# A transformer layer on one core: the first block's heads turned by VectorE instead of TensorE, and three pieces of work near the start given other places

## The chip, the cores and the metric

One core of a Trainium2 chip runs the whole kernel in one launch. The metric is the time of one execution on the device in microseconds (us). The engines are named as the profile names them: PE is TensorE (PEld its weight loads), DVE is VectorE, ACT is ScalarE, POOL is GpSimd, and SP is the sync engine, which here does nothing but issue most of the DMA transfers.

## The reference: what is computed

One decoder layer over 256 tokens of width 2048, in float32. After an RMSNorm, one wide input projection gives the columns of two attention groups: eight heads of sparse attention (queries, and keys and values for a compressed, a selected and a windowed branch, with sigmoid gates per head and branch) and four heads of differential attention. The part that matters here is the start of the first group:

```python
k_cmp = compress_blocks(apply_rope(k_c.reshape(b, t_len, g, dh), cos, sin), cmp_pos, cmp_k_w1, cmp_k_w2)
v_cmp = compress_blocks(v_c.reshape(b, t_len, g, dh), cmp_pos, cmp_v_w1, cmp_v_w2)
...
blocks = jnp.transpose(blocks, (0, 1, 3, 2, 4)).reshape(b, n_cmp, g, CMP_BLOCK * dh)
return jax.nn.silu(blocks @ w1) @ w2
```

Both groups' outputs are multiplied by a SiLU branch, concatenated, sent through an output projection and added to the input, and a final RMSNorm follows.

## The kernel before, in words

**The work as a stream.** The projections are cut into column blocks of 512, and each block into four chunks: a chunk is four 128 x 512 tiles of weights (1 MB). The weights of the two compressions (`ck`, `cv`) are cut in chunks of the same size. The list `STREAM` (lines 54 to 62) is the order in which PE takes all chunks; it is written out by hand, and everything else is placed by numbers that name a chunk of this list. Its beginning before the change, with the chunk number c: c0 to c7 are the chunks of input blocks 0 (`kc`, `vc`: keys and values to be compressed) and 1 (`ks`, `kw`: the two other branches' keys) mixed; c8 and c9 the first two chunks of block 2 (`vs`, `vw`: their values); c10 to c13 the first four chunks of `ck`; c14 and c15 the other two of block 2; c16 and c17 block 3; c18 to c21 the rest of `ck`.

**A projection chunk.** For each tile of weights `w` the kernel makes a rounded high part `whi` (ACT, line 487) and the rest `wlo = w - whi` (DVE, line 786), and PE adds up three products, `whi*x_hi`, `wlo*x_hi` and `whi*x_lo` (lines 1191 to 1193; lines 1230 to 1237 in the first five chunks), for two tiles of 128 tokens: 24 matmuls of 512 columns a chunk. PE takes a chunk only when its high and its low part are there (lines 1173, 1174). ACT and DVE each run one loop over c: in turn c they split the chunk two places further on in the list of projection chunks, so in turn 7 the one for c9, and in turn 8 the next after that (c14 before the change). There are four raw buffers and three split buffers; SP reloads a raw buffer when both parts of the chunk that was in it are made (lines 382, 383), in the order of the list `LOADS`. A compression chunk isn't split: 16 matmuls of 512 columns with 32 columns of weights each (line 1250), 0.9 us in place of 5.4 us.

**All engines keep to the order of their own program.** What stands in an engine's turn c runs in that order, and a wait holds up everything behind it on that engine.

**Block 0.** In turn 6 ACT takes its values into `stage` (line 530), DVE scales the sine and cosine tables by the token norm (line 1032) and takes the keys with rotary embedding in two parts (lines 838 to 841), and POOL adds the two parts (line 437, one instruction for each tile of tokens). After chunk 7 PE transposes the eight 128 x 128 squares into the PSUM banks `S` (line 1269), ACT copies them out to `kvcT` in turn 8 (line 545), and DVE adds the position vector to form `kblkf` in turn 8 and `vblkf` in turn 13 (line 1054), with which PE begins `ck` and `cv`.

**Block 1** is a head block: DVE applies the rotary embedding when it is done (turn 7 and the start of turn 8), POOL adds, and DVE turns its heads in turns 9 and 10 into `kaT` with 16 stream transposes of 32 rows (line 850); these wait for the gate products, since `kaT` lies where `xTs` was. **Block 2** holds values: ACT takes the high part (line 539), DVE the low one (line 910), after c15.

**The gates.** DVE forms `gw` from the gate weights `gwf` in turn 7 (line 1061), PE multiplies after c9 (line 1276, 32 small matmuls), ACT copies the result out (line 706).

Of the kernel before, what the change touches and what calls it, by code (L numbers as in the profile page):

```python
# [24 lines left out]
P = 128  # L25
D_MODEL, SEQ, HEAD = 2048, 256, 128
TT = SEQ // P
KT = D_MODEL // P
# [14 lines left out]
for _n, _w in (("qa", 1024), ("kc", 256), ("vc", 256), ("ks", 256), ("vs", 256), ("kw", 256), ("vw", 256),  # L43
# [3 lines left out]
N_GATE = 24  # L47
BLOCKS = [("kc", "vc"), ("ks", "kw"), ("vs", "vw"), ("qa", 0), ("qa", 1), ("qb", 0), ("kb", 0), ("qb", 1),
          ("kb", 1), ("vb", 0), ("vb", 1), ("za", 0), ("za", 1), ("zb", 0), ("zb", 1)]
# [6 lines left out]
STREAM = [("in", b, j) for b, j in ((0, 0), (1, 0), (0, 1), (1, 1), (0, 2), (0, 3), (1, 2), (1, 3))] + _in[8:9]  # L56
for _i in range(0, 16, 4):

    STREAM += _in[9 + max(_i - 3, 0):10 + _i] + _cmp[_i:_i + 4]
STREAM += _in[22:24]  # L60
# [9 lines left out]

ROPE = [0, 1, 3, 4, 5, 6, 7, 8]
HEADS_AT = {b: {0: 7}.get(b, LAST["in", b] + 2) for b in ROPE}
Z = [11, 12, 13, 14]
# [3 lines left out]
SQ = 32  # L77
GATE_AT, GATE_TURN = 9, 17
CMP_SCORES_AT, CMP_PROBS_AT = 39, 45
# [43 lines left out]
def program(nc, stream, w_gate, head, x, norm_w, cmp_pos, ck_w2, cv_w2, lam, subln_w, final_w, consts, out):  # L123
# [3 lines left out]
    with ExitStack() as ctx:  # L127
# [134 lines left out]
        rope_ready = sem("rope_ready")  # L262
        kvc_turned, kvc_taken = sem("kvc_turned"), sem("kvc_taken")
        heads_turned, z_turned = sem("heads_turned"), sem("z_turned")
# [23 lines left out]
        READERS = {b: "v" for b in range(N_IN + N_OUT)}  # L288
        READERS.update({0: "vs", 2: "sv", 9: "sv", 10: "sv", 11: "s", 12: "s", 13: "s", 14: "s"})

# [4 lines left out]
        def values(b, t):  # L295

            at = slice(0, NB) if b == 2 else slice((b - 9) * NB, (b - 8) * NB)
            return [m[:, t, at] for m in ((va, va_lo) if b == 2 else (vb, vb_lo))]

# [177 lines left out]
        def _(act):  # L477
# [55 lines left out]
            def take_v(b, t):  # L533

                a = use_done(b, t)
                if b == 9:
                    act.wait_ge(scores_done, TT * N_A)
                dst = values(b, t)[0]
                act.activation(dst, a[:, :], ACT.Copy, scale=rstd[:, t:t + 1]).then_inc(acc_read["s"], 1)

            def take_kvc():

                for t in range(TT):
                    act.wait_ge(kvc_turned, t + 1)
                    act.activation(kvcT[:, :, t * P:(t + 1) * P], S[:, 1 + t, :].rearrange("p (h q) -> p h q", h=4), ACT.Copy)\
                        .then_inc(kvc_taken, 1)

# [112 lines left out]
            def take(c, t):  # L660

                for b in (2, 9, 10):
                    if c == LAST["in", b]:
                        take_v(b, t)
                for b in range(11, N_IN):
                    if c == LAST["in", b]:
                        silu_z(b, t)

            for c in range(N_CHUNKS):
# [15 lines left out]
                if c == 4:  # L685
                    act.dma_start(const[:, :], consts).then_inc(const_in, 16)
                    act.dma_start(posT[:, :], cmp_pos).then_inc(const_in, 16)
                    act.dma_start(gwf[:, :, :], w_gate).then_inc(gw_in, 16)
                if c == HEADS_AT[0] + 1:
                    take_kvc()  # L690
                if c == 7:
# [81 lines left out]
        def _(dve):  # L773
# [46 lines left out]
            def rope(b, t):  # L820
# [6 lines left out]
                if n > 1:  # L827
                    dve.wait_ge(heads_turned, turned(ROPE[n - 1]))
                elif n:
                    dve.wait_ge(kvc_turned, t + 1)  # L830
                else:

                    dve.wait_ge(acc_read["s"], t + 1)
# [19 lines left out]
            def turn_heads(b, rows):  # L853
                n = ROPE.index(b)
                if rows[0] == 0:
                    dve.wait_ge(rope_ready, TT * (n + 1))
                    if b == 1:
                        dve.wait_ge(g_done, 1)
                    if b == 5:
                        dve.wait_ge(hid_done, 2)  # L860
                dst = {1: kaT[:, :, :], 3: qaT[:, 0:4, :], 4: qaT[:, 4:8, :], 5: qbT[:, 0:4, :],
                       6: kbT[:, 0:4, :], 7: qbT[:, 4:8, :], 8: kbT[:, 4:8, :]}[b]
                turn(dst, rows, heads_turned)

            def turn_z(b, rows):
# [35 lines left out]
            def take_v_lo(b, t):  # L901

                a = use_done(b, t)
                hi, lo = values(b, t)
                dve.wait_ge(acc_read["s"], reads("s", TT * b + t + 1))
                if b == 2:
                    dve.wait_ge(x_squared, TT)
                else:
                    dve.wait_ge(scores_done, TT * N_A)
                dve.scalar_tensor_tensor(lo, a[:, :], rstd[:, t:t + 1], hi.bitcast(f32), ALU.mult, ALU.subtract)\  # L910
                    .then_inc(acc_read["v"], 1)
# [83 lines left out]
            def take(c, t):  # L995

                for b in ROPE[1:]:
                    if c == LAST["in", b]:
                        rope(b, t)
                for b in (2, 9, 10):  # L1000
                    if c == LAST["in", b]:
                        take_v_lo(b, t)
                for n in range(N_OUT - 1):
                    if c == LAST["out", n]:
                        residual(n, t)

            start(0)
            for c in range(N_CHUNKS):
# [14 lines left out]
                for u in range(N_UNITS):  # L1023
                    if c == UNIT_AT[u] + 4:
                        take_pT_lo(u)
                if c == 6:

                    dve.wait_ge(rstd_steps, 2)
# [16 lines left out]
                if c == LAST["in", Z[-1]] + 2:  # L1045
                    turn_z(Z[-1], range(2, 4))
                for k, w in enumerate(("ck", "cv")):
                    if c == (8, 13)[k]:

                        dve.wait_ge(kvc_taken, TT)  # L1050
                        dve.wait_ge(blk_zero, 2)
# [4 lines left out]
                                          ALU.add).then_inc(blk_sum, 1)  # L1056
                if c == 7:
                    dve.wait_ge(gw_in, 16)
                    dve.wait_ge(blk_zero, 3)
                    dve.wait_ge(nw_in, 16)  # L1060
                    dve.tensor_tensor(gw[:, :, 0:N_GATE], gwf[:, :, :], nw[:, :].unsqueeze(2).to_broadcast([P, KT, N_GATE]),
                                      ALU.mult).then_inc(gw_ready, 1)
                if c == LAM_AT + 4:
# [96 lines left out]
        def _(pe):  # L1160
# [101 lines left out]

            def turn_kvc():
                pe.wait_ge(const_in, 32)
                for t in range(TT):
                    pe.wait_ge(rope_ready, t + 1)
                    pe.wait_ge(acc_read["s"], t + 1)
                    for h in range(4):
                        last = pe.transpose(S[:, 1 + t, h * P:(h + 1) * P], stage[:, t, h * P:(h + 1) * P], ident)
                    last.then_inc(kvc_turned, 1)  # L1270

            def gate_products():
# [6 lines left out]

            def turn_gates():  # L1280
                pe.wait_ge(g_taken, 1)
                pe.wait_ge(kvc_taken, TT)
                banks_free()
# [163 lines left out]
            for c in range(N_CHUNKS - SPLIT):  # L1447
                if STREAM[c][0] in ("ck", "cv"):
                    products_cmp(c)
                else:  # L1450
                    products(c)
                if c == HEADS_AT[0]:
                    turn_kvc()
                if c == GATE_AT:
# [102 lines left out]
```

## Time and profile before

| | |
|---|---|
| median of 3 runs | 486.46 us (486.42 to 486.58) |
| the profiled execution's own time | 486.59 us |
| its span, first to last instruction | 484.8 us |
| around the span | 1.79 us |
| PE busy | 476.3 us, 98% |
| DVE busy | 355.7 us, 73% |
| ACT busy | 233.6 us, 48% |
| POOL busy | 45.8 us, 9% |
| mean granted clock of PE | 0.995 |

Matmuls overlap in the records: one of 512 columns is shown as 0.39 us long, while the next starts 0.227 us after it. How long PE takes is therefore read from starts, not from durations. The same holds in a small way on DVE and ACT, where an instruction starts some 0.08 us before the end of the one before it.

### The profile page before, as it was taken

Reading aid. Unit: us, or ns where it says so; the run is one execution under the profiler, and the core shown is the slowest. Engines: PE = TensorE matmul, PEld = TensorE weight load, DVE = VectorE, ACT = ScalarE, POOL = GpSimd, SP = SyncE. Lnnn points to the kernel's source line nnn. Section 1 sums busy time; section 2 is a strip of 40 time slices with the busy share of each in tenths; the row PEclk is TensorE's granted clock in tenths of the full one; section 3 lists DMA queues with packets and bytes.
Section 4 is the critical chain, followed back from the end, with each engine's and each line's share of the span. In section 5 each row is a group of like instructions: output and inputs, shape, how many; then the busy total and the mean of one; then the engine's idle time right before and its main releaser. Section 6 shows DMA issues by size and latency. Waiting matters only on the chain.

```text
span 484.8 us, 6561 instructions
## 1 busy us (share of the span) xinstructions
PE 476.3 (98%) x2574; PEld 389.5 (80%) x2574; DVE 355.7 (73%) x477; ACT 233.6 (48%) x336; POOL 45.8 (9%) x49
## 2 busy tenths in 40 slices
PE   9999999999999999999999999999999999999994
PEld 8888868686868888888888888888888888888883
DVE  5855896468778799998978656588897998454533
ACT  6847525233334465846547455554436443534331
POOL 1003400020202002020200000102000000303050
PEclk9999999999999999999999999999999999999998
DMA  8999999888945435244453524345775355655004
GB/s 270 417 421 413 414 415 370 326 339 318 369 174 190 159 110 179 82 175 173 174 174 97 187 96 178 149 173 218 287 276 196 155 183 205 240 218 192 1 0 174
DMA packets 18734, 107.71 MB, mean 222 GB/s; under 512 B 2320, under 2 KB 2960, under 8 KB 7440
## 3 DMA queue, kind: packets, MB, share of 16 engines
q1 hardware_dynamic: 17264, 104.34, 56.9%
q10 hardware_dynamic: 1440, 2.96, 1.6%
q8 instruction: 20, 0.33, 0.3%
q14 instruction: 10, 0.08, 0.0%
HBM read 105.20 MB, written 2.10 MB: 221 GB/s over the span
## 4 chain that ended last, share of the span: by engine, by line
PE 98%; issue 0%; DVE 0%; POOLq 0%; DVEq 0%; ACT 0%; POOL 0%; ACTq 0%
PE acc L1191 26%; PE acc L1193 26%; PE acc L1192 26%; PE O L1250 3%; PE acc L1230 2%; PE acc L1233 2%; PE acc L1237 2%; PE S L1382 1%; PE S L1367 1%; PE acc L1446 1%; PE S L1355 1%; PE O L1405 1%; PE O L1406 1%; PE O L1404 1%; PE O L1416 1%; PE S L1356 1%
## 5 line engine op out<-in xcount | busy, mean ns | idle before, releaser
L786 DVE TENSOR_TENSOR wlo<-raw,whi 128x2048 fp32r<-128x2048 f32 x71 | 164.4, 2318 | 84.4 <-ACT whi L487 84.0
L487 ACT ACTIVATE whi<-raw 128x2048 fp32r<-128x2048 f32 x71 | 136.0, 1916 | 139.8 <-PE acc L1193 128.9
L1191 PE MATMUL acc<-whi,hT_hi 128*128 128x512 f32 x432 | 170.0, 394 | 0.0
L1193 PE MATMUL acc<-whi,hT_lo 128*128 128x512 f32 x432 | 168.3, 390 | 0.0
L1192 PE MATMUL acc<-wlo,hT_hi 128*128 128x512 f32 x432 | 168.1, 389 | 0.0
L1191 PEld LDWEIGHTS acc<-whi,hT_hi 128*128 128x128 f32 x432 | 81.1, 188 | 19.9 <-issue 3.4
L1193 PEld LDWEIGHTS acc<-whi,hT_lo 128*128 128x128 f32 x432 | 81.1, 188 | 17.2
L1192 PEld LDWEIGHTS acc<-wlo,hT_hi 128*128 128x128 f32 x432 | 81.2, 188 | 16.4
L437 POOL TENSOR_TENSOR stage<-stage,stage 128x512 f32<-128x512 f32 (+1 forms) x16 | 23.4, 1478 | 174.0 <-DVE stage L841 174.0
L582 ACT ACTIVATE e<-S,small 128x128 f32<-128x128 f32 (+1 forms) x48 | 19.5, 419 | 21.4 <-DVE small L899 21.4
L850 DVE STREAM_TRANSPOSE zT<-stage 32x256 f32<-32x256 f32 x64 | 27.9, 436 | 2.0
L1191 PE MATMUL acc<-whi,mixA_hi 128*128 128x512 f32 x64 | 24.9, 389 | 0.0
L1192 PE MATMUL acc<-wlo,mixA_hi 128*128 128x512 f32 x64 | 24.9, 389 | 0.0
L1193 PE MATMUL acc<-whi,mixA_lo 128*128 128x512 f32 x64 | 24.9, 389 | 0.0
L1191 PE MATMUL acc<-whi,mixB_hi 128*128 128x512 f32 x60 | 23.3, 389 | 0.0
L1192 PE MATMUL acc<-wlo,mixB_hi 128*128 128x512 f32 x60 | 23.3, 389 | 0.0
L1193 PE MATMUL acc<-whi,mixB_lo 128*128 128x512 f32 x60 | 23.3, 389 | 0.0
L461 POOL TENSOR_TENSOR x_nat<-x_nat,fw 128x512 f32<-128x512 f32 x6 | 11.9, 2003 | 120.9 <-ACT junk L647 120.9
L813 DVE TENSOR_TENSOR wlo<-raw,whi 128x512 fp32r<-128x512 f32 (+1 forms) x14 | 12.7, 918 | 3.0 <-ACT whi L498 2.8
L850 DVE STREAM_TRANSPOSE qaT<-stage 32x256 f32<-32x256 f32 x32 | 13.9, 436 | 0.9
L850 DVE STREAM_TRANSPOSE kbT<-stage 32x256 f32<-32x256 f32 x32 | 13.9, 435 | 0.9
L850 DVE STREAM_TRANSPOSE qbT<-stage 32x256 f32<-32x256 f32 x32 | 13.9, 435 | 0.9
(202 smaller groups left out, 536.7 us busy)
## 6 DMA issues: line engine op xcount, KB each, us to landing
raw<-stream SPq DMA_DIRECT2D x71, 1024.0 KB, 4.8
row_raw<-stream SPq DMA_DIRECT2D x8, 1024.0 KB, 7.9
row_x<-stream SPq DMA_DIRECT2D x4, 1024.0 KB, 10.3
raw<-head SPq DMA_DIRECT2D x6, 512.0 KB, 8.3
raw<-head SPq DMA_DIRECT2D x8, 256.0 KB, 5.1
x_nat<-x_rows SPq DMA_DIRECT2D x2, 1024.0 KB, 14.8
row_x<-stream SPq DMA_DIRECT2D x4, 512.0 KB, 10.7
row<-stream SPq DMA_DIRECT2D x4, 512.0 KB, 12.0
```

The lines of the kernel that those rows point to most:

```text
L437: pool.tensor_tensor(stage[:, t, 0:w], stage[:, t, 0:w], stage2[:, t, 0:w], ALU.add)\
L461: pool.tensor_tensor(y, y, fw[:, n * NB:(n + 1) * NB], ALU.mult).then_inc(yw_ready, 1)
L487: act.activation(whi[:, n % SPLIT, :], raw[:, n % RAW, :], ACT.Copy).then_inc(hi_ready, 1)
L582: act.activation((e0 if t == 0 else e1)[:, i, :], src, ACT.Exp, bias=nmax[:, 4 * t + i:4 * t + i + 1], accum_out=sums[:, 4 * t + i:4 * t + ...
L786: dve.tensor_tensor(wlo[:, n % SPLIT, :], raw[:, n % RAW, :], whi[:, n % SPLIT, :].bitcast(f32), ALU.subtract)\
L813: dve.tensor_tensor(wlo[:, c2 % SPLIT, at], raw[:, c2 % RAW, at], whi[:, c2 % SPLIT, at].bitcast(f32), ALU.subtract).then_inc(lo_ready if ...
L850: dve.transpose(out[:, :, :, SQ * i:SQ * (i + 1)], src[:, :, :, SQ * j:SQ * (j + 1)])\
L1191: pe.matmul(acc_bank(n), xh, wh, start=k == 0, stop=False)
L1192: pe.matmul(acc_bank(n), xh, wl, start=False, stop=False)
L1193: last = pe.matmul(acc_bank(n), xl, wh, start=False, stop=k == KT - 1)
L1230: pe.matmul(acc_bank(TT * b + t), xh[t], wh, start=k == 0, stop=False)
L1250: last = pe.matmul(O[32 * i:32 * (i + 1), k, :], blkf[kind][:, CH * j + i, :, :].rearrange("p g n -> p (g n)"), row_of(c, i), start=j == 0 ...
```

## The change

The order of blocks becomes (`kc`,`vc`), (`vs`,`vw`), (`ks`,`kw`): the values are now block 1 and are finished at c7, the other keys are block 2 and are finished at c15. In `STREAM` a third chunk of block 2 comes ahead of the compression, so c10 is a projection chunk and the first four `ck` chunks are c11 to c14; from c15 on the kinds of chunk are as before. The squares of block 0 are turned by DVE with its stream transposes, eight in turn 6 and eight in turn 7, directly into `kvcT`; PE's transposes and ACT's copy are gone. `gw` is formed first thing in turn 6, the gate products come after c7, and their result is copied in ACT's turn 8. The values of block 1 are written where `xTs` lies, so ACT waits for the gate products before it takes them. The heads of block 2 are turned in turns 17 and 18.

```diff
-BLOCKS = [("kc", "vc"), ("ks", "kw"), ("vs", "vw"), ("qa", 0), ("qa", 1), ("qb", 0), ("kb", 0), ("qb", 1),
+BLOCKS = [("kc", "vc"), ("vs", "vw"), ("ks", "kw"), ("qa", 0), ("qa", 1), ("qb", 0), ("kb", 0), ("qb", 1),
...
-for _i in range(0, 16, 4):
-
-    STREAM += _in[9 + max(_i - 3, 0):10 + _i] + _cmp[_i:_i + 4]
+for _i, (_a, _b) in zip(range(0, 16, 4), ((9, 11), (11, 14), (14, 18), (18, 22))):
+    STREAM += _in[_a:_b] + _cmp[_i:_i + 4]
...
-ROPE = [0, 1, 3, 4, 5, 6, 7, 8]
-HEADS_AT = {b: {0: 7}.get(b, LAST["in", b] + 2) for b in ROPE}
+ROPE = [0, 2, 3, 4, 5, 6, 7, 8]
+HEADS_AT = {b: {0: 6}.get(b, LAST["in", b] + 2) for b in ROPE}
...
-GATE_AT, GATE_TURN = 9, 17
+GATE_AT, GATE_TURN = 7, 17
...
             def take_v(b, t):
 
                 a = use_done(b, t)
+                if b == 1:
+                    act.wait_ge(g_done, 1)
...
-            def take_kvc():
-
-                for t in range(TT):
-                    act.wait_ge(kvc_turned, t + 1)
-                    act.activation(kvcT[:, :, t * P:(t + 1) * P], S[:, 1 + t, :].rearrange("p (h q) -> p h q", h=4), ACT.Copy)\
-                        .then_inc(kvc_taken, 1)
...
+            def turn_kvc(rows):
+
+                dve.wait_ge(rope_ready, TT)
+                dve.wait_ge(acc_read["s"], TT)
+                turn(kvcT, rows, kvc_turned)
...
                 if c == 6:
+                    dve.wait_ge(gw_in, 16)
+                    dve.wait_ge(blk_zero, 3)
+                    dve.wait_ge(nw_in, 16)
+                    dve.tensor_tensor(gw[:, :, 0:N_GATE], gwf[:, :, :], nw[:, :].unsqueeze(2).to_broadcast([P, KT, N_GATE]),
+                                      ALU.mult).then_inc(gw_ready, 1)
+                if c == 6:
...
+                if c == HEADS_AT[0]:
+                    turn_kvc(range(0, 2))
+                if c == HEADS_AT[0] + 1:
+                    turn_kvc(range(2, 4))
                 for k, w in enumerate(("ck", "cv")):
                     if c == (8, 13)[k]:
 
-                        dve.wait_ge(kvc_taken, TT)
+                        dve.wait_ge(kvc_turned, SQ // 2)
...
-            def turn_kvc():
-                pe.wait_ge(const_in, 32)
-                for t in range(TT):
-                    pe.wait_ge(rope_ready, t + 1)
-                    pe.wait_ge(acc_read["s"], t + 1)
-                    for h in range(4):
-                        last = pe.transpose(S[:, 1 + t, h * P:(h + 1) * P], stage[:, t, h * P:(h + 1) * P], ident)
-                    last.then_inc(kvc_turned, 1)
```

The remaining lines of the diff rename block 2 to block 1 where values are meant and block 1 to block 2 where heads are meant, and drop the semaphore `kvc_taken`. In DVE's turns 6 and 7 the new turns stand behind the split of the next chunk's low part.

## Rows read from the trace of the kernel before

**Rows 1.** The page: busy time and share, then granted clock and DMA, 40 slices.
```profile
PE 476.3 (98%) x2574; PEld 389.5 (80%) x2574; DVE 355.7 (73%) x477; ACT 233.6 (48%) x336; POOL 45.8 (9%) x49
...
PEclk9999999999999999999999999999999999999998
DMA  8999999888945435244453524345775355655004
```
**Rows 2.** The waits, PE alone: engine, line, waited for, total us, times, longest.
```profile
PE acc L1446 <- DVE warm L780: 1.0, 1, 1.0
```
**Rows 3.** Timeline of DVE, 44 to 72 us: start, length, line, tiles, count, [idle <-releaser].
```profile
44.07 0.74 DVE L1032 TENSOR_SCALAR const<-const,small 128x64 f32<-128x64 f32 x4 [3.08 <-POOL small L430]
...
46.35 2.33 DVE L786 TENSOR_TENSOR wlo<-raw,whi 128x2048 fp32r<-128x2048 f32 x1
50.13 2.29 DVE L786 TENSOR_TENSOR wlo<-raw,whi 128x2048 fp32r<-128x2048 f32 x1 [1.44 <-ACT whi L487]
52.34 0.55 DVE L1061 TENSOR_TENSOR gw<-gwf,nw 128x384 f32<-128x384 f32 x1
52.81 0.68 DVE L838 SCALAR_TENSOR_TENSOR stage<-acc,const 128x512 f32<-128x512 f32 x1
...
55.33 2.35 DVE L786 TENSOR_TENSOR wlo<-raw,whi 128x2048 fp32r<-128x2048 f32 x1
57.60 2.88 DVE L1054 TENSOR_TENSOR kblkf<-kvcT,posT 128x960 f32<-128x960 f32 x1
60.39 2.27 DVE L786 TENSOR_TENSOR wlo<-raw,whi 128x2048 fp32r<-128x2048 f32 x1
62.89 7.44 DVE L850 STREAM_TRANSPOSE kaT<-stage 32x256 f32<-32x256 f32 x16 [0.23 <-PE O L1276]
70.37 1.86 DVE L1054 TENSOR_TENSOR vblkf<-kvcT,posT 128x960 f32<-128x960 f32 x1
```
**Rows 4.** Timeline of PE, 43 to 50.3 us: chunk 7, transposes, chunk 8.
```profile
43.37 0.39 PE L1191 MATMUL acc<-whi,hT_hi 128*128 128x512 f32 x1
...
48.58 0.40 PE L1193 MATMUL S<-whi,hT_lo 128*128 128x512 f32 x1
48.82 1.18 PE L1269 MATMUL S<-const,stage 128*128 128x128 f32 x8
49.75 0.48 PE L1191 MATMUL acc<-whi,hT_hi 128*128 128x512 f32 x1
50.07 0.40 PE L1192 MATMUL acc<-wlo,hT_hi 128*128 128x512 f32 x1
```
**Rows 5.** Timeline of PE, 60 to 66.5 us: gate products and first `ck` chunks.
```profile
60.50 0.39 PE L1193 MATMUL acc<-whi,hT_lo 128*128 128x512 f32 x1
60.82 1.93 PE L1276 MATMUL O<-xTs,gw 128*32 128x256 f32 x32
62.57 1.90 PE L1250 MATMUL O<-row_raw,kblkf 128*32 128x512 f32 x16
...
66.12 0.50 PE L1191 MATMUL acc<-whi,hT_hi 128*128 128x512 f32 x1
66.45 0.40 PE L1192 MATMUL acc<-wlo,hT_hi 128*128 128x512 f32 x1
```
**Rows 6.** The transfer of the gate weights, by its tile `gwf`.
```profile
L688 ACTq DMA_DIRECT2D gwf<-w_gate x1: 453/453/453, 32.3 to 32.3; - x1
...
DMA to landing us min/median/max: 12.1/12.1/12.1
```
**Rows 7.** Timeline of POOL, 46.7 to 48 us: second tile of block 0.
```profile
46.52 2.76 POOL L437 TENSOR_TENSOR stage<-stage,stage 128x256 f32<-128x256 f32 x1
```
**Rows 8.** DVE taking low parts of block 2's values (line 910).
```profile
L910 DVE SCALAR_TENSOR_TENSOR va_lo<-acc,small,va_hi x2: 747/749/751, 76.6 to 78.1; 128x512 fp32r<-128x512 f32 x2
```
**Rows 9.** Timeline of ACT, 50 to 63 us.
```profile
50.67 1.92 ACT L487 ACTIVATE whi<-raw 128x2048 fp32r<-128x2048 f32 x1 [0.57 <-DMA raw<-stream]
52.49 1.07 ACT L545 ACTIVATE kvcT<-S 128x512 f32<-128x512 f32 x2
```
**Rows 10.** Timeline of SP, 60 to 70 us, and PE's next `ck` chunks.
```profile
62.74 0.33 SPq L389 DMA_DIRECT2D raw<-stream  x1
63.67 1.84 SPq L379 DMA_DIRECT2D row_raw<-stream  x2
...
88.25 0.62 PE L1250 MATMUL O<-row_raw,kblkf 128*32 128x512 f32 x4
```
**Rows 11.** DMA issues, 63 to 70 us: count, size, us to landing.
```profile
row<-stream SPq DMA_DIRECT2D x1, 512.0 KB, 12.9
```
**Rows 12.** Stretches at the kernel's end: us, PE, PEld, DVE, ACT, POOL, granted clock, DMA.
```profile
478.00:480.00 2.00, 0.00 (x0) 0.00 (x0) 1.42 (x5) 0.35 (x1) 0.94 (x1) 1.00 0.01 4
480.00:482.00 2.00, 0.00 (x0) 0.00 (x0) 1.03 (x3) 0.37 (x1) 0.00 (x0) 0.60 0.39 152
```
**Rows 13.** Landings of stream loads issued between 12 and 70 us (line 389).
```profile
DMA to landing us min/median/max: 6.7/13.0/17.4
```

More of the change, by code:

```diff
@@ L262, in program @@
         rope_ready = sem("rope_ready")
-        kvc_turned, kvc_taken = sem("kvc_turned"), sem("kvc_taken")
+        kvc_turned = sem("kvc_turned")
         heads_turned, z_turned = sem("heads_turned"), sem("z_turned")
@@ L288, in program @@
         READERS = {b: "v" for b in range(N_IN + N_OUT)}
-        READERS.update({0: "vs", 2: "sv", 9: "sv", 10: "sv", 11: "s", 12: "s", 13: "s", 14: "s"})
+        READERS.update({0: "vs", 1: "sv", 9: "sv", 10: "sv", 11: "s", 12: "s", 13: "s", 14: "s"})
         def reads(engine, uses):
@@ L295, in values @@
         def values(b, t):
-            at = slice(0, NB) if b == 2 else slice((b - 9) * NB, (b - 8) * NB)
-            return [m[:, t, at] for m in ((va, va_lo) if b == 2 else (vb, vb_lo))]
+            at = slice(0, NB) if b == 1 else slice((b - 9) * NB, (b - 8) * NB)
+            return [m[:, t, at] for m in ((va, va_lo) if b == 1 else (vb, vb_lo))]
         def row_parts(c):
@@ L660, in take @@
             def take(c, t):
-                for b in (2, 9, 10):
+                for b in (1, 9, 10):
                     if c == LAST["in", b]:
@@ L688, in _ @@
                     act.dma_start(gwf[:, :, :], w_gate).then_inc(gw_in, 16)
-                if c == HEADS_AT[0] + 1:
-                    take_kvc()
                 if c == 7:
@@ L829, in rope @@
                 elif n:
-                    dve.wait_ge(kvc_turned, t + 1)
+                    dve.wait_ge(kvc_turned, SQ // 2)
                 else:
@@ L856, in turn_heads @@
                     dve.wait_ge(rope_ready, TT * (n + 1))
-                    if b == 1:
+                    if b == 2:
                         dve.wait_ge(g_done, 1)
@@ L860, in turn_heads @@
                         dve.wait_ge(hid_done, 2)
-                dst = {1: kaT[:, :, :], 3: qaT[:, 0:4, :], 4: qaT[:, 4:8, :], 5: qbT[:, 0:4, :],
+                dst = {2: kaT[:, :, :], 3: qaT[:, 0:4, :], 4: qaT[:, 4:8, :], 5: qbT[:, 0:4, :],
                        6: kbT[:, 0:4, :], 7: qbT[:, 4:8, :], 8: kbT[:, 4:8, :]}[b]
                 turn(dst, rows, heads_turned)
+            def turn_kvc(rows):
+                dve.wait_ge(rope_ready, TT)
+                dve.wait_ge(acc_read["s"], TT)
+                turn(kvcT, rows, kvc_turned)
             def turn_z(b, rows):
@@ L905, in take_v_lo @@
                 dve.wait_ge(acc_read["s"], reads("s", TT * b + t + 1))
-                if b == 2:
+                if b == 1:
                     dve.wait_ge(x_squared, TT)
@@ L999, in take @@
                         rope(b, t)
-                for b in (2, 9, 10):
+                for b in (1, 9, 10):
                     if c == LAST["in", b]:
@@ L1046, in _ @@
                     turn_z(Z[-1], range(2, 4))
+                if c == HEADS_AT[0]:
+                    turn_kvc(range(0, 2))
+                if c == HEADS_AT[0] + 1:
+                    turn_kvc(range(2, 4))
                 for k, w in enumerate(("ck", "cv")):
                     if c == (8, 13)[k]:
-                        dve.wait_ge(kvc_taken, TT)
+                        dve.wait_ge(kvc_turned, SQ // 2)
                         dve.wait_ge(blk_zero, 2)
@@ L1056, in _ @@
                                           ALU.add).then_inc(blk_sum, 1)
[L1057 to L1062, printed above, removed]
                 if c == LAM_AT + 4:
@@ L1280, in turn_gates @@
             def turn_gates():
+                pe.wait_ge(const_in, 32)
                 pe.wait_ge(g_taken, 1)
-                pe.wait_ge(kvc_taken, TT)
                 banks_free()
@@ L1451, in _ @@
                     products(c)
-                if c == HEADS_AT[0]:
-                    turn_kvc()
                 if c == GATE_AT:
```

## The prediction

> **What bounds the kernel now.** I read the page first: PE is busy for 98% of the span, DVE for 73%, and PE's granted clock is at its upper level, 2.4 GHz, throughout [rows 1]. Then the waits of PE alone: one, for the warm-up tile at 1.0 us [rows 2]. So nothing after the start makes PE wait for long, and the time is the sum of what PE is given to do. Two things follow. Work taken off PE is won in full; and the time that any other engine makes PE wait is lost in full, since nothing later catches up. The busy share of DVE says little here. What counts is its timeline between 44 and 64 us against PE's, which is where the change puts work, and there DVE has only short gaps: 3.08 us before the tables, 1.44 us before the second split, then back to back from 50.13 to 62.66 us [rows 3]. The DMA engines are full in that stretch too, at eight or nine tenths up to slice 10 [rows 1].
>
> All times below are of the profiled execution, whose own time is 486.59 us; it lies 0.13 us above the median of the three runs, 486.46 us. About 0.2% (1 us) is what a measurement of this kernel can tell from no change.
>
> **What PE is spared.** Chunk 7 starts at 43.37 us and its last matmul at 48.58 us; with starts 0.227 us apart it leaves PE at 48.81 us, 5.44 us for 24 matmuls. Without the eight transposes the second matmul of chunk 8 would start at 48.58 + 2 x 0.227 = 49.03 us; it starts at 50.07 us [rows 4]. That is 1.04 us, with the switch into and out of the transposes in it.
>
> **What the moved gates cost PE.** Today the gate products stand between chunk 9 and the first compression chunk: they start 0.09 us late (60.82 for 60.73 us) and take 1.75 us until line 1250 starts, and there is no switch between the two kinds of small matmul. Going back to wide ones costs 0.10 us (66.12 to 66.45 us, less 0.227) [rows 5]. After the change wide products follow the gates and a compression follows wide products, so there is one more way out and one more way in: +0.10 + 0.09 = 0.19 us. **PE's own work shrinks by 1.04 - 0.19 = 0.85 us.** The swap of blocks and the compression that comes a chunk later change no count of matmuls.
>
> **What PE then needs, and when.** Chunk 7 ends at 48.81, the gates run to 48.90 + 1.75 = 50.65, chunk 8 (with 0.10 for the switch) to 56.19, chunk 9 to 61.63 us. Then comes chunk 10, which is new here: today the compression stands at this place, which needs no split, and the low part of the third chunk of block 2, made from 55.33 us on [rows 3], is not wanted before 66.12 us [rows 5]. That cover is gone.
>
> **DVE's line, step by step.**
> - `gw` now stands ahead of the tables. It needs `gwf`, issued at 32.30 us and landed 12.1 us later, at 44.40 us [rows 6]; the instruction holds DVE for 52.81 - 52.34 = 0.47 us [rows 3]. The tables start at 44.87 in place of 44.07 us: everything behind is 0.80 us later. Had `gwf` landed by 43.6 us this would cost nothing.
> - Split of chunk 8: ends at 48.68 + 0.80 = 49.48 us, ahead of PE at 50.65 us.
> - First eight turns: they wait for both of POOL's sums. POOL's second sum took 2.76 us and ended at 49.28 us, 0.60 us after DVE's split had ended [rows 3, 7]. Both move by 0.80 us, so the sums end at 50.08 us and DVE, done with its split, stands still for 0.6 us. Sixteen turns of the same shape took 70.37 - 62.89 = 7.48 us with the hand-over [rows 3]. Eight: 3.74 us, to 53.8 us.
> - Split of chunk 9, queued behind them: 2.21 us (50.13 to 52.34) [rows 3], to 56.05 us. PE wants it at 56.19 us: just in time.
> - Second eight turns: to 59.8 us.
> - Low parts of block 1's values, twice 0.75 us [rows 8] less overlap, 1.4 us: to 61.2 us. In place of these DVE had two rotary takes (52.81 to 55.33 us) [rows 3].
> - Split of chunk 10: 2.3 us, to 63.5 us.
>
> PE wants it at 61.63 us: **PE waits 1.9 us**. What is queued behind on DVE is `kblkf` (1.9 to 2.9 us [rows 3]), done by 66.4 us and wanted at 63.5 + 5.44 = 69 us, and the splits for chunks 15 and 16, to 71.0 us; chunk 15 starts at 69.0 + 0.09 + 3.55 = 72.7 us. So the wait happens once. Later DVE gets the two rotary takes and the turns of block 2 in turns 15 to 18; before a projection chunk that PE takes in 5.44 us DVE has one split of 2.3 us to make, and turns 18 to 21 are compression chunks with no split, so I take nothing for it.
>
> **ACT, SP and POOL.** ACT loses the copy out of PSUM, 1.07 us [rows 9], and gets nothing new; its value takes wait for the gates at 50.65 us, and the high part of chunk 10 queued behind, today made at 50.67 us [rows 9], comes at some 54 us, before DVE asks for it at 61.2 us. Nothing. On SP one more stream load now stands ahead of the loads of `ck` chunks 18 to 21, and it waits for the low part of chunk 16: they go out near 70.5 in place of 63.67 us [rows 10]. The slowest of them landed after 12.9 us [rows 11], so by 84 us, and PE wants them at 88.25 + 1.05 us [rows 10]: 5 us of cover, nothing. Without that cover every us of delay would be a us of the total. POOL has the same sums.
>
> **The sum.** -0.85 + 1.9 = +1.05 us on 486.59 us, 487.64 us; on the median's footing **487.5 us**. The unknown inside is how PE resumes after a wait: between nothing and the 0.10 us of a switch [rows 5]; I take nothing, since weights can be loaded during the wait, and a gain is excluded, as waiting removes no matmul. The clock: after PE's last matmul the row from 478 to 480 us still shows 1.00 with PE idle, and only the next shows 0.60 [rows 12], so a single wait under 2 us should leave 2.4 GHz in place.
>
> The 7.48 us for sixteen turns carries the result. The Trainium skill, in "VectorE: DVE Perf Modes", section "The three transpose paths", gives VectorE 311 ns for a 128 x 128 bf16 square in 32 x 32 blocks and TensorE 390 ns. By that, eight squares would be 2.5 us of DVE time, an estimate from the page; the row has the same sort of block at f32 and in 32-row instructions, three times as long, and the row decides. With 2.5 us the sum would be -0.85 us.
>
> **Rivals.**
> 1. *DVE keeps up; only PE's saving is left.* It decides where DVE's chain to the split of chunk 10 is at least 1.9 us shorter than I have it: turns of 0.35 us in place of 0.467, or `gw` free (0.8) together with shorter standing for POOL (0.6) and overlap. For it: the margin is small against a 17 us chain. Against it: every step has its row with the same shape. Time: 486.46 - 0.85 = 485.6 us, which is "same" by 0.2% and not slower.
> 2. *The wait is longer, from `gwf`.* With the DMA engines full, landings of stream loads spread from 6.7 to 17.4 us [rows 13], and `gwf` now gates the tables, the rotary take, the turns and three splits. Each us of delay is a us at chunk 10; 1.5 us later also makes PE wait at chunk 8. Time: 487.5 + 1.5 = 489.0 us. Against it: DMA traffic before 44 us is unchanged.
> 3. *SP's later loads run dry.* The 5 us of cover above would have to go; then PE waits at chunk 18. Time: 2 us more, 489.5 us.
> 4. *It is really faster, by over 1 us.* PE's saving is bounded by 1.04 us even if switches were free, so this needs something that no row shows.
>
> **How the numbers follow.** The forecast (one wait of 1.3 to 2.5 us at chunk 10): 0.57, 486.9 to 488.1 us. Rival 1, waits of 0 to 1.2 us: 0.21. Rival 2: 0.12. Rival 3: 0.04. Rival 4: 0.06. The forecast lies nearly on the 0.2% line (487.43 us), so I halve it: slower 0.31 + 0.12 + 0.04 = 0.47; same 0.26 + 0.21 = 0.47; faster 0.06. The range runs from rival 1's end to rival 2's, 485.5 to 489.0 us; the likeliest case's own range is the 486.9 to 488.1 above.
>
> **What would show it.** In the profile after: no line of PE transposes before 50 us, the gate products starting at 48.9 us; the tables of line 1032 at 44.9 us behind `gw`, released by the transfer of `gwf`; the first `kvcT` turn at 50.1 us released by POOL; the split of chunk 10 (line 786) ending near 63.5 us, and a wait of PE for it of 1.9 us in the list of waits, from 61.6 us on. Wrong would be: no wait of PE on `wlo`, kvcT turns well under 0.467 us apart, or a wait at another chunk (8, 9, 15 or 18), and a fall of the granted clock after 61.6 us.

## The result, and the profile after

The changed kernel took **487.91 us** (median of 11 runs, 487.28 to 488.55) against 486.58 us (11 runs of the kernel before beside it, 486.20 to 487.74). The ratio is 1.0026, 95% interval 1.0019 to 1.0034: slower by 1.3 us, where +1.05 us was forecast. The profiled execution took 487.28 us, with a span of 485.1 us.

The page of the changed kernel, the lines that answer to [rows 1]:

```profile
PE 475.1 (98%) x2566; PEld 387.7 (80%) x2566; DVE 362.2 (75%) x493; ACT 232.5 (48%) x334; POOL 43.8 (9%) x49
...
PEclk9999999999999999999999999999999999999998
```

Its waits of PE alone, which answer to [rows 2] (engine, line, waited for, total us, times, longest):

```profile
PE acc L1193 <- DVE wlo L778: 1.2, 1, 1.2
PE acc L1439 <- DVE warm L772: 1.0, 1, 1.0
PE acc L1232 <- ACT whi L495: 0.2, 1, 0.2
```

Eight matmuls fewer on PE, sixteen instructions more on DVE, and one new wait that counts: PE waits 1.2 us for a low part that DVE makes. (The 0.2 us for ACT's `whi` are at PE's first wide matmul; such a wait comes and goes between kernels that are equal there.) DVE's busy share rose by two points only, and nothing in that share tells that DVE now sets the pace at one place. PE's timeline shows where (to be read against [rows 4, 5]): the gates directly after chunk 7, and the hole ahead of chunk 10.

```profile
48.00 0.39 PE L1195 MATMUL S<-whi,hT_lo 128*128 128x512 f32 x1
48.32 1.93 PE L1269 MATMUL O<-xTs,gw 128*32 128x256 f32 x32
50.18 0.50 PE L1193 MATMUL acc<-whi,hT_hi 128*128 128x512 f32 x1
50.52 0.40 PE L1194 MATMUL acc<-wlo,hT_hi 128*128 128x512 f32 x1
...
60.97 0.39 PE L1195 MATMUL acc<-whi,hT_lo 128*128 128x512 f32 x1
62.59 0.47 PE L1193 MATMUL acc<-whi,hT_hi 128*128 128x512 f32 x1 [1.24 <-DVE wlo L778]
62.90 0.40 PE L1194 MATMUL acc<-wlo,hT_hi 128*128 128x512 f32 x1
```

From start to start the hole is 62.59 - 60.97 - 0.23 = 1.39 us; the list of waits counts 1.24 us of it, since the last matmul's record still runs. DVE's timeline in the same stretch, which answers to [rows 3], is the chain behind it:

```profile
43.37 0.56 DVE L1028 TENSOR_TENSOR gw<-gwf,nw 128x384 f32<-128x384 f32 x1 [3.40 <-DMA gwf<-w_gate]
43.84 0.74 DVE L1036 TENSOR_SCALAR const<-const,small 128x64 f32<-128x64 f32 x4
...
46.08 2.33 DVE L778 TENSOR_TENSOR wlo<-raw,whi 128x2048 fp32r<-128x2048 f32 x1
49.03 3.71 DVE L842 STREAM_TRANSPOSE kvcT<-stage 32x256 f32<-32x256 f32 x8 [0.63 <-POOL stage L436]
52.77 2.29 DVE L778 TENSOR_TENSOR wlo<-raw,whi 128x2048 fp32r<-128x2048 f32 x1
55.09 3.71 DVE L842 STREAM_TRANSPOSE kvcT<-stage 32x256 f32<-32x256 f32 x8
58.84 0.75 DVE L908 SCALAR_TENSOR_TENSOR va_lo<-acc,small,va_hi 128x512 fp32r<-128x512 f32 x1
59.51 0.74 DVE L908 SCALAR_TENSOR_TENSOR va_lo<-S,small,va_hi 128x512 fp32r<-128x512 f32 x1
60.17 2.28 DVE L778 TENSOR_TENSOR wlo<-raw,whi 128x2048 fp32r<-128x2048 f32 x1
62.37 1.86 DVE L1062 TENSOR_TENSOR kblkf<-kvcT,posT 128x960 f32<-128x960 f32 x1
```

The split of chunk 10 ends at 62.45 us, 19.1 us after `gw` began, and PE goes on 0.14 us later. Everything between is back to back but for the 0.63 us in which DVE stands for POOL.

**A measure that leaves the start out.** From PE's first wide matmul to the end of chunk 7 the profiled executions differ by up to 1.1 us from one to the next (43.4 to 44.6 us between the first start and that of chunk 7's last matmul), in kernels that are equal up to there. So the traces are compared below by the time from the start of chunk 7's last matmul to the start of the very last one. In the kernel before that is 477.25 - 48.58 = 428.67 us, and 428.54 and 428.57 us in two kernels that differ from it in idle DVE instructions alone; in the changed kernel 477.53 - 48.00 = 429.53 us, and 429.67 us in a second profile. **The change costs PE's line 1.0 us** (the mean of its two traces, 429.60, less that of the three others, 428.59). The rest of the measured 1.3 us is found outside the span; more on that at the end.

### The profile page after: what moved, and what is told of

Same layout as the page of the kernel before. It is cut to its first block, busy times and chain, and to the rows that moved or that the text cites. A ratio compares the mean times of both kernels' runs of the same rounds, so it can differ in the third digit from the quotient of the medians.

```text
span 485.1 us, 6560 instructions
## 1 busy us (share of the span) xinstructions
PE 475.1 (98%) x2566; PEld 387.7 (80%) x2566; DVE 362.2 (75%) x493; ACT 232.5 (48%) x334; POOL 43.8 (9%) x49
## 4 chain that ended last, share of the span: by engine, by line
PE 85%; DMA 5%; DVE 4%; ACT 2%; issue 1%; SPq 1%; POOL 1%; POOLq 0%; DVEq 0%; ACTq 0%
PE acc L1193 25%; PE acc L1195 25%; PE acc L1194 25%; DMA raw<-stream 3%; PE O L1252 3%; DMA raw<-head 1%; PE S L1375 1%; DVE kvcT L842 1%; PE S L1360 1%; DVE wlo L805 1%; DVE wlo L778 1%; POOL stage L436 1%; SPq L366 1%; ACT whi L486 1%; PE S L1348 1%
## 5 line engine op out<-in xcount | busy, mean ns | idle before, releaser
L436 POOL TENSOR_TENSOR stage<-stage,stage 128x512 f32<-128x512 f32 (+1 forms) x16 | 21.4, 1352 | 177.3 <-DVE stage L833 177.3
```

Source lines behind the costliest of these rows:

```text
L436: pool.tensor_tensor(stage[:, t, 0:w], stage[:, t, 0:w], stage2[:, t, 0:w], ALU.add)\
```

## The experiments

The theory: DVE's line from the landing of the gate weights to the split of chunk 10 sets when PE may take chunk 10; PE's own saving is real but smaller than that wait. The rivals: the new order with its switches between kinds of matmul costs the time, or the transposes were worth nothing.

**Less ahead of the turns: `gw` after the split.**

```diff
-                if c == 6:
-                    dve.wait_ge(gw_in, 16)
...
                     split_lo(HALVED[PLACE[c] + 2])
...
+                if c == 6:
+                    dve.wait_ge(gw_in, 16)
...
                 if c == HEADS_AT[0]:
                     turn_kvc(range(0, 2))
```

> The changed kernel, but DVE forms gw in turn 6 after the split of chunk 8 and ahead of the first turns, where it stands still 0.63 us for POOL. Theory (DVE's line sets the end of the split of chunk 10, and each us on it is a us of PE's wait): everything behind the tables comes 0.8 us sooner, PE's wait at chunk 10 falls from 1.24 us (as the list of waits counts it) to some 0.4 us, and the time falls by about 0.8 us, to 487.1 us. Rival (the loss is in the new order of PE's work, its switches between kinds of matmul): no change, 487.9 us.

487.37 us (11 runs) against 486.65 us (33 runs of the kernel before on the same chip), ratio 1.0015 (1.0006 to 1.0023): 0.7 us over the kernel before in place of 1.3 us. Apart from the warm-up, PE's list of waits of this kernel has two entries in place of one:

```profile
PE O L1269 <- DVE gw L1049: 0.4, 1, 0.4
PE acc L1193 <- DVE wlo L778: 0.4, 1, 0.4
```

The wait at chunk 10 fell from 1.2 to 0.4 us as expected, but the expectation had left out who waits for `gw` itself: PE came to the gates 0.4 us before it was there. The measure from chunk 7 on is 478.27 - 49.16 = 429.11 us, 0.5 us under the changed kernel. `gw` also took longer than expected in this place, as DVE's timeline of this kernel shows:

```profile
48.82 1.09 DVE L1049 TENSOR_TENSOR gw<-gwf,nw 128x384 f32<-128x384 f32 x1
49.83 3.70 DVE L842 STREAM_TRANSPOSE kvcT<-stage 32x256 f32<-32x256 f32 x8
```

It took 1.09 us, against 0.56 us in the changed kernel. POOL's timeline of the same execution has the second sum until 46.73 + 2.77 = 49.5 us:

```profile
46.73 2.77 POOL L436 TENSOR_TENSOR stage<-stage,stage 128x256 f32<-128x256 f32 x1
```

The Trainium skill, "SBUF — State Buffer", section "Who interferes with whom", says that a VectorE instruction with two SBUF inputs contends with a GpSimd instruction that reads SBUF, and calls the port pair that they share an exclusive lock. The traces agree from both sides: POOL's second sum took 2.76 us and ended 0.60 us after the split beside it [rows 3, 7], where the first one, 0.74 us long, had no split beside it; and `kblkf` took 2.88 us from 57.60 us on [rows 3], beside a sum that ran until 58.82 us, and took 1.86 us in the changed kernel's timeline above, with no sum beside it. The gap in which DVE waits for POOL was thus no free place for an instruction of this kind.

**The second eight turns later.**

```diff
-                if c == HEADS_AT[0] + 1:
+                if c == HEADS_AT[0] + 2:
                     turn_kvc(range(2, 4))
```

> The changed kernel, but DVE does the second eight turns in turn 8, after the split of chunk 10, instead of in turn 7. Theory: the split of chunk 10 ends 3.7 us sooner, 2.5 us ahead of PE, and kblkf still comes 2 us ahead of chunk 11, so PE never waits; left is PE's own saving, 1.04 us of transposes less 0.34 us of switches: 0.7 us under the kernel before, 485.9 us. Rival (switches and order cost as much as the transposes did): at or over 486.6 us though the wait is gone.

486.27 us (11 runs) against 486.65 us, ratio 0.9994 (0.9985 to 1.0002). No wait on `wlo` is left in PE's list:

```profile
PE acc L1439 <- DVE warm L772: 1.0, 1, 1.0
```

The measure from chunk 7 on is 477.01 - 49.02 = 427.99 us, 0.6 us under the kernel before and 1.6 us under the changed one. This is the decisive one: the same work on the same engines, one group of eight instructions moved behind one split, takes the loss away, and what is left is PE's saving, a little under the 0.7 us expected. The median of the times is 0.38 us under the kernel before, and its interval does not exclude no change; some 0.37 us more around the span (last section) stand against the saving.

**Both.** The two edits together.

> Both edits: gw in the gap and the second eight turns after the split of chunk 10. Theory: with no wait of PE left, DVE's 0.8 us are worth nothing more; 485.9 us, the same as with the turns alone. Rival (there is a further hidden wait on DVE somewhere behind): under the kernel with the late turns by 0.3 us or more.

486.76 us (11 runs), ratio 1.0006 (0.9998 to 1.0015). By the medians that is 0.5 us more than with the late turns alone, though the two intervals overlap, and 477.15 - 48.92 = 428.23 us in the measure, 0.24 us more. Neither theory nor rival had it longer. No wait after chunk 7 is long enough for the list, but DVE's timeline has it:

```profile
48.27 1.09 DVE L1049 TENSOR_TENSOR gw<-gwf,nw 128x384 f32<-128x384 f32 x1
```

`gw` is there at 49.36 us, and PE's gates start at 49.42 us, 0.18 us behind 48.92 + 0.23 + 0.09 = 49.24 us. It is the wait of the first experiment again, and shorter, and it explains most of the 0.24 us of the traces; that the rest of the 0.5 us comes from it too is not shown. The rival, a further wait on DVE, would have made it faster. As far as the traces tell, once nothing behind `gw` is late, its early place is the better one by some 0.2 us.

**The new order with PE's turns.** DVE's turns taken out, PE's transposes and ACT's copy put back, directly ahead of the gate products.

```diff
-                if c == HEADS_AT[0]:
-                    turn_kvc(range(0, 2))
-                if c == HEADS_AT[0] + 1:
-                    turn_kvc(range(2, 4))
...
+                if c == 7:
+                    turn_kvc()
                 if c == GATE_AT:
                     gate_products()
```

> The changed kernel's stream order, early gw and early gate products, but the first block is turned by PE and copied out by ACT as before (transposes straight ahead of the gate products). Theory: no wait of PE; the order alone costs only switches between kinds of matmul, 0.1 to 0.3 us: 486.7 to 486.9 us. Rival (the order itself, with the compression a chunk later, gains or loses more): outside 486.3 to 487.2 us.

487.45 us (11 runs), ratio 1.0018 (1.0009 to 1.0027), outside the bounds that the rival was given. The trace, though, doesn't put it on the order. PE's timeline of this kernel:

```profile
48.37 0.60 PE L1270 MATMUL S<-const,stage 128*128 128x128 f32 x4
49.83 0.66 PE L1270 MATMUL S<-const,stage 128*128 128x128 f32 x4 [0.86 <-POOL stage L436]
50.41 1.93 PE L1277 MATMUL O<-xTs,gw 128*32 128x256 f32 x32
```

The second tile's squares wait 0.86 us for POOL's sum. With `gw` ahead of the tables the rotary take and the sums come late, and here it is PE that stands behind them. To see whether that was all, `gw` was moved after the split of chunk 8 in this kernel too, with the edit of the first experiment:

> The kernel with PE's turns in the new order, with gw formed after the split of chunk 8 instead of ahead of the tables. There PE waited 0.9 us for POOL's sum at the transposes. Theory (that wait was the 0.8 us by which gw ahead of the tables and the rotary take delays the sums): it falls to 0.1 to 0.3 us, and the time from 487.45 to 486.7 us. Rival (the order of the stream costs this time itself): 487.4 us.

486.86 us (11 runs) against 486.80 us (33 runs), ratio 1.0005 (0.9996 to 1.0014), and PE's timeline has the transposes without a hole:

```profile
48.83 1.04 PE L1270 MATMUL S<-const,stage 128*128 128x128 f32 x8
49.80 1.93 PE L1277 MATMUL O<-xTs,gw 128*32 128x256 f32 x32
```

So the order costs little: 477.49 - 48.60 = 428.89 us in the measure, 0.2 to 0.3 us over the kernel before, about what its switches come to (0.34 us, worked out below). And `gw` ahead of the tables cost 0.9 us of waiting here, where PE stood next behind the sums; set against the kernel before on the same chip, the two medians are 0.7 us apart.

**DVE's turns in the old order.** The kernel before with DVE's turns in turns 6 and 7 behind the splits, and nothing else of the change.

```diff
+                if c == 6:
+                    turn_kvc(range(0, 2))
+                if c == 7:
+                    turn_kvc(range(2, 4))
                 for k, w in enumerate(("ck", "cv")):
                     if c == (8, 13)[k]:
-                        dve.wait_ge(kvc_taken, TT)
+                        dve.wait_ge(kvc_turned, SQ // 2)
```

> The kernel before with one part of the change alone: DVE turns the first block in turns 6 and 7, all else (order of the stream, gates, block 1 with its heads) as before. Theory: DVE's line becomes the bound here too, at two places: the split of chunk 9 ends near 55.3 us where PE wants it at 54.3, a wait of about 1 us, and kblkf, behind the two rotary takes and the next split, ends near 67 us where PE wants it at 62.6, a wait of about 4.6 us; with 1.04 us of transposes saved, 4.7 us slower than before, 491.3 us. Rival (DVE has room, the reordering was not needed): 0.9 us faster than before, 485.6 us.

493.67 us (4 runs) against 486.75 us (7 runs), ratio 1.0144 (1.0127 to 1.0161): 6.9 us slower. The two waits are where and about as long as expected, 1.0 us for the split of chunk 9 and 4.2 us for `kblkf`:

```profile
PE O L1251 <- DVE kblkf L1055: 4.2, 1, 4.2
PE acc L1438 <- DVE warm L771: 1.0, 1, 1.0
PE acc L1192 <- DVE wlo L777: 1.0, 1, 1.0
```

Waits of 5.2 us less the 1.0 us of transposes would give 4.2 us, and 6.9 us were measured. The stretches of this kernel (us, then PE, PEld, DVE, ACT and POOL busy, granted clock, DMA share, GB/s) show the larger part of the rest:

```profile
64.00:66.00 2.00, 0.00 (x0) 0.00 (x0) 2.00 (x2) 1.41 (x1) 1.66 (x1) 1.00 0.29 33
66.00:68.00 2.00, 0.64 (x4) 0.23 (x8) 2.00 (x2) 0.00 (x0) 0.00 (x0) 0.68 0.85 352
68.00:70.00 2.00, 2.00 (x16) 0.55 (x12) 1.97 (x3) 0.00 (x0) 0.00 (x0) 0.50 0.33 139
70.00:72.00 2.00, 2.00 (x24) 0.53 (x16) 1.87 (x5) 0.00 (x0) 0.00 (x0) 0.97 0.69 225
```

PE's timeline there:

```profile
67.36 3.27 PE L1251 MATMUL O<-row_raw,kblkf 128*32 128x512 f32 x16 [4.21 <-DVE kblkf L1055]
70.45 1.47 PE L1251 MATMUL O<-row_x,kblkf 128*32 128x512 f32 x10
```

While PE stood, its granted clock fell to 0.50, the level of 1.2 GHz, and the sixteen small matmuls behind took 3.27 us in place of 1.90 [rows 5], 1.4 us more. Most of the remaining 1.3 us can be found as well. 0.37 us are around the span (last section). Another 0.37 us are a hole ahead of chunk 8, which starts at 48.87 us and not at 48.27 + 0.23 us: its split ends at 48.77 us, and the transposes that covered this are gone. And the two waits are longer from start to start than in the list, since the records of the last matmuls still run: chunk 9 starts at 55.57 us and the matmul before it at 54.16, so the hole is 55.57 - 54.16 - 0.23 = 1.18 us, and the first `ck` chunk starts 67.36 - 61.22 - 1.75 = 4.39 us late behind the gates. That is 0.35 us more. Some 0.2 us are left, most of it in getting going behind the holes. In the changed kernel the row from 62 to 64 us, in which its wait of 1.24 us ends, still has 1.00:

```profile
62.00:64.00 2.00, 1.41 (x6) 1.22 (x7) 2.00 (x2) 1.36 (x1) 0.00 (x0) 1.00 0.22 41
```

What this experiment tells of the change: the swap of blocks and the third chunk ahead of the compression are what makes room for DVE's turns, 16.3 us of PE's time (three chunks) instead of 10.9 us between the end of chunk 7 and the first use of `kblkf`, gates not counted. The order isn't the loss; without it DVE's turns cost five times as much.

**The changed kernel again.**

> The changed kernel again, for a second profile. Theory: the wait at chunk 10 is the distance between the landing of the gate weights, with 18.8 us of DVE work behind it, and PE's own progress, so it is again between 1.2 and 2.2 us, and moves one for one with the start of gw less the end of chunk 7. Rival: the wait is another size with the same distance.

487.64 us, one run, and a wait of 1.4 us at chunk 10. `gw` starts at 43.80 and chunk 7's last matmul at 48.26 us, 4.46 us apart, against 48.00 - 43.37 = 4.63 us before: 0.17 us closer, and the measure is 429.67 for 429.53 us, 0.14 us longer. Two points are few, but they lie as a race between the landing of `gwf` and PE's progress would have them. In the other three kernels with `gw` first the distance is 4.73 us (late turns), 4.45 us (late turns with the semaphore) and 3.98 us (PE's turns, new order), so it scatters by 0.75 us among five executions that are equal up to there.

**The dropped semaphore.** For the time around the span, told of in the last section, the kernel with the late turns was run with one line changed.

```diff
-        kvc_turned = sem("kvc_turned")
+        kvc_turned, kvc_taken = sem("kvc_turned"), sem("kvc_taken")
```

> The kernel with the late turns, with the semaphore that the change dropped (kvc_taken) declared again and used by nothing. In the runs so far the time minus the span is 1.80 us in the kernels that have it (before, and the one with PE's turns in the new order) and 2.17 us in those that don't. Theory (the time around the span depends on what is declared, by way of this semaphore): 1.80 us around the span, 485.9 us. Rival (it depends on DVE's program, which has 16 instructions more): 2.17 us around it, 486.3 us. The span itself stays at 484.1 us by both.

The time around the span stayed at 2.17 us (486.44 us of 11 runs against 486.80 us, ratio 0.9997, 0.9988 to 1.0005); its trace repeats the late turns' result, 476.51 - 48.51 = 428.00 us.

**Late gates as well.** The kernel with late turns, with these edits:

```diff
-GATE_AT, GATE_TURN = 7, 17
+GATE_AT, GATE_TURN = 10, 17
...
                 for b in (1, 9, 10):
-                    if c == LAST["in", b]:
+                    if c == (10 if b == 1 else LAST["in", b]):
                         take_v_lo(b, t)
```

the same for ACT's take, and `gw` in turn 9.

> The kernel with the late turns, and the gates back ahead of the compression: gate products after chunk 10, gw in turn 9, the takes of block 1's values (ACT and DVE) in turns 10 and 11. Theory: the two switches of PE that the early gates cost (0.34 us by the changed kernel's rows) go away, no wait comes in their place, and since gw no longer stands ahead of the tables DVE's line is 0.8 us shorter still: 0.34 us under the kernel with the late turns, 485.9 us. Rival (switches cost nothing of their own, the 0.34 us lie elsewhere): 486.3 us.

486.81 us (11 runs), ratio 1.0007 (0.9998 to 1.0016): no better than with the gates early, and PE's timeline has a new wait:

```profile
54.34 0.39 PE L1195 MATMUL acc<-whi,hT_lo 128*128 128x512 f32 x1
55.67 0.47 PE L1193 MATMUL acc<-whi,hT_hi 128*128 128x512 f32 x1 [0.94 <-DVE wlo L778]
```

PE now waits 0.94 us ahead of chunk 9. What the expectation missed is that the early gates are more than work: their 1.86 us (48.32 to 50.18 us above) lie between chunk 7 and chunk 8 and give DVE time for the first eight turns. Their cost of a third of a microsecond in switches buys that cover. So with the gates late, four of the first eight turns have to go too:

```diff
-                if c == HEADS_AT[0]:
-                    turn_kvc(range(0, 2))
+                if c in (HEADS_AT[0], HEADS_AT[0] + 1):
+                    turn_kvc(range(c - HEADS_AT[0], c - HEADS_AT[0] + 1))
```

> The kernel with late turns and late gates, with the sixteen turns spread as four in turn 6, four in turn 7 and eight in turn 8 behind the split of chunk 10. With the gates late PE wants the split of chunk 9 1.9 us sooner, at 54.5 us, and eight turns ahead of it made PE wait 0.9 us there. Theory: with four turns less ahead of it that split ends near 53.4 us, the split of chunk 10 near 57.6 (wanted at 60), kblkf near 63.5 (wanted at 67): no wait of PE, no further switch, so PE's part after chunk 7 is 1.04 us less than in the kernel before; with 2.17 us around the span, 0.7 us under the kernel before, 486.0 us. Rival (some other wait comes, of POOL's or of the raw loads): 486.3 us or more.

486.14 us (11 runs) against 486.61 us (21 runs), ratio 0.9992 (0.9983 to 1.0001): the lowest ratio of all, yet not clear of no change. Its trace measures 476.32 - 48.44 = 427.88 us, 0.7 us under the kernel before and 1.7 us under the changed one, with no wait listed after the start. DVE's timeline of this kernel:

```profile
48.53 1.83 DVE L842 STREAM_TRANSPOSE kvcT<-stage 32x256 f32<-32x256 f32 x4 [0.64 <-POOL stage L436]
50.39 2.29 DVE L778 TENSOR_TENSOR wlo<-raw,whi 128x2048 fp32r<-128x2048 f32 x1
52.72 1.83 DVE L842 STREAM_TRANSPOSE kvcT<-stage 32x256 f32<-32x256 f32 x4
54.58 2.29 DVE L778 TENSOR_TENSOR wlo<-raw,whi 128x2048 fp32r<-128x2048 f32 x1
56.91 3.72 DVE L842 STREAM_TRANSPOSE kvcT<-stage 32x256 f32<-32x256 f32 x8
...
64.65 0.56 DVE L1063 TENSOR_TENSOR gw<-gwf,nw 128x384 f32<-128x384 f32 x1
```

Of the expected 1.04 us some 0.3 us are missing. About 0.2 us of them can be seen: `gw` ends at 65.21 us, and PE's gates start at 65.27 us, 0.28 us behind the earliest start after chunk 10 (64.76 + 0.23 us), where the same switch is 0.09 us in the kernel before [rows 5]. A turn sooner for `gw` should give that back; it wasn't tried.

## Why the prediction was right

**The bound and the wait.** Right in kind and place: PE never waited for long before, and now waits once, at chunk 10, for DVE's low part. That moving eight turns behind that split takes the wait and the loss away was shown by the kernel with the late turns.

**DVE's line**, from the start of `gw` to the end of chunk 10's split, was put at 63.5 - 44.4 = 19.1 us; it is 62.45 - 43.37 = 19.1 us. Its terms hold one by one: 0.47 us for `gw`; 0.63 us of standing for POOL (0.6 said); 3.74 us for eight turns, from 49.03 to 52.77 us; 1.33 us for the two value takes (1.4 said).

**The size of the wait** was put at 1.9 us and came out at 1.39 us from start to start, and 0.1 us for getting going again, near the lower end of the likeliest case's own 1.3 to 2.5 us. The step that was off is not the chain but where it is fastened: the landing of `gwf` was taken at 44.40 us with chunk 7's last matmul at 48.58, 4.18 us apart, from one execution of the kernel before; in the profile after they are 4.63 us apart, so 0.45 us of the wait are gone. This distance varies by itself, from 3.98 to 4.73 us in the five executions above, and the forecast took one value of it. Two smaller terms nearly cancel: PE left the gates 0.13 us later than forecast, and took up chunk 10 0.14 us after its split had ended, where nothing was set down for this. The phrase "a 17 us chain" in the first rival is a slip: the prediction's own steps make 19.1 us.

**PE's saving.** 1.04 us for the transposes stands. The switches were put at 0.19 us, and cost more: out of the gates 0.23 us (50.98 to be compared with 48.32 + 1.75 + 3 x 0.227 = 50.75 us), and 0.09 us into the first compression chunk. Together with 0.02 us in the compression that is 0.34 us, so PE's own saving is 0.7 us and not 0.85; the late turns, where nothing waits, measure it at 0.6 us. That the kernel with PE's turns and `gw` moved is 0.2 to 0.3 us longer than the one before in the traces agrees with it.

**The sum.** With a saving of 0.6 to 0.7 us and a wait of 1.5 us, PE's line is 0.8 to 0.9 us longer by this account; the profiled execution's trace has 0.94 us and the mean of the two traces 1.0 us, against +1.05 said. The total came out 0.3 us higher than the traces' difference, from a source that the forecast did not have. So the direction and the mechanism were forecast, but that +1.05 and +1.3 us lie so close is partly luck: the wait was put 0.4 us too long, the saving about 0.2 us too large, and 0.37 us around the span were not foreseen, and these misses offset each other.

**The rivals.** DVE does not keep up: its turns are 0.467 us apart as said. At f32 and in sixteen 32-row instructions the eight squares took 2 x 3.74 us. By the figure of the Trainium skill, "VectorE: DVE Perf Modes", section "The three transpose paths", 311 ns for a bf16 square, they would take 2.5 us, an estimate, and leave no wait; the measurement decides. The late landing of `gwf` is a part of the picture in small, 0.17 us between two profiles, and not 1.5 us. SP's loads were delayed as worked out, the `ck` loads of chunks 18 to 21 went out at 69.38 us (70.5 said), and made nobody wait. "Nothing" for the clock was right for this wait, and would have been wrong for the one of 4.2 us in the old order.

## What to carry to other kernels

On a kernel whose bound engine never waits, ask of each moved instruction which deadline stands behind it in its queue, rather than what share of the engine is busy. Eight instructions put behind one split were worth 1.6 us. Work of the bound engine can be cover for another, as the gates were: moving it changes the deadlines of every engine that feeds the chunks around it. And a wait long enough to lower PE's clock costs more than its length: 1.4 us on top of 4.2 us here.

## What was not expected of the hardware

**The time around the span has levels.** The time of an execution less its span is 1.80 us in the median for the kernel before (33 runs, 1.76 to 1.85 us), and 2.18 us for the changed kernel (11 runs, 2.13 to 2.22): 0.37 us, more than a quarter of the measured loss, in which no instruction of the profile runs. The spans are on record to 0.1 us, so a spread of 0.05 us to either side is rounding. The level belongs to the kernel and not to the execution:

| kernel | time around the span, us | DVE instructions against before | `kvc_taken` declared |
|---|---|---|---|
| before | 1.80 | | yes |
| PE's turns, new order (both) | 1.81, 1.81 | 0 | yes |
| changed | 2.18 | +16 | no |
| `gw` in the gap; late turns; both; turns in the old order; late gates | 2.15 to 2.17 | +16 | no |
| late turns, semaphore declared | 2.17 | +16 | yes |
| turns spread 4, 4, 8 | 1.82 | +16 | no |
| before, 16 memsets more | 2.01 | +16 | yes |
| before, 48 memsets more | 1.79 | +48 | yes |

The kernels with memsets have this edit, with 16 or 48:

```diff
+                if c == 22:
+                    for i in range(16):
+                        dve.memset(idle[:, i:i + 1], 0.0)
```

> The kernel before with 16 more instructions on DVE, memsets of one column each in turn 22 where DVE is idle for 6 us. Theory (the time around the span goes by the semaphore): 1.80 us around the span, 486.65 us. Rival (it goes by the length of DVE's program): 2.17 us around it, 487.0 us.

486.77 us (10 runs), ratio 1.0004 (0.9995 to 1.0013).

> The kernel before with 48 more memsets on DVE in its idle turn 22 instead of 16 (which raised the time around the span from 1.80 to 2.01 us). If the time around the span goes with the number of DVE's instructions, 0.2 us for 16, it is 2.4 us here. If it is a step, 2.0 to 2.2 us.

486.58 us (8 runs), ratio 1.0000 (0.9990 to 1.0010). The dropped semaphore is not the cause, as declaring it again changed nothing, and neither is the length of DVE's program: 48 instructions more left the level as it was, 16 more raised it half-way (to a level that neither the theory nor the rival had), and the spread turns have as many instructions as the changed kernel and the lower level. What sets it stays open. For a comparison of a few tenths of a microsecond it is a reason to look at spans beside times.

**The clock after a wait of 4.2 us.** One such wait brought PE from 2.4 to 1.2 GHz and made the work behind it 1.4 us longer, while the wait of 1.24 us left it at 2.4 GHz. No run here has a wait of a length between the two.
